# Sixteen input slabs of a hybrid decoder layer become fill work between the steps of its recurrences

## The chip, the cores and the metric

One core of a Trainium2 chip runs the whole program in one launch. The metric is device time in microseconds; three runs of the kernel before gave a median of 2457.02 us (2455.21 to 2465.17).

## The reference, cut to what matters

Two layers over 512 prompt tokens and 8 decode tokens (520 columns, always carried together). A layer first mixes tokens:

```python
h = rmsnorm(x, norm1_g)
z = h @ w_in                                   # 57 column groups of 128 here
mq, mk, mv, mi, mf, mo, gq, gk, gv, glr, go, pu, gates = split_cols(z)
hm, C1, n1, m1 = mlstm_chunked(q, k, v, i_pre, logf, C0, n0, m0)   # needs mq mk mv mi mf
y_ml  = head_rmsnorm(hm, ml_g) * sigmoid(mo)
og, S1 = gla_chunked(q2, k2, v2, log_a, S0)                        # needs gq gk gv glr
y_gla = head_rmsnorm(og, gla_g) * silu(go)
y_pool, buf1 = pool_mixer(pu, buf0, pos0, pool_w, pool_scale)      # needs pu
proj  = einsum('btnc,ncd->btnd', stack([y_ml, y_gla, y_pool]), w_branch)
x = x + sum(sigmoid(gates) * proj) @ w_out
```

and then channels: a dense SwiGLU in layer 0, a top-2-of-8 mixture of experts in layer 1. All is float32.

## The kernel before, in words

Activations lie with the feature on the partition and the 520 tokens along the free axis. A weight is streamed from HBM in slabs of 1024 by 128 (512 KB). ScalarE copies a slab to a rounded part `w_hi` (`split_hi`), VectorE subtracts to get the remainder `w_lo` (`split_lo`), and TensorE forms hi*hi + hi*lo + lo*hi, that is 48 matmuls of 260 columns per slab, into one of two PSUM places (`out_ps`). There are four places for raw slabs and three for split ones, and a slab is split two slabs ahead of its use. SyncE loads the slabs, in order, and stores the gates (below) in between.

The 57 slabs of `w_in` come in this order: 1 with the small gates and the low-rank part, 2 gk, 2 gq, 4 gv, then 4 q, 4 k, 4 v, 4 pooling inputs, then 32 gates (mo, go, 24 branch gates). Before, the first 25 run back to back (`inputs`): VectorE reads each result from PSUM, multiplies it by the row norm `rs` and writes its buffer. The remaining 32 are *fill slabs*: in the program of every engine a call `fill(k)` stands between the steps of the recurrences and does k half slabs of its share of the work. On TensorE that is 24 matmuls; on ScalarE, at every second half, the split of the slab two ahead and the copy of the slab before it out of PSUM into `sq`; on VectorE the subtraction. SyncE stores `sq` to DRAM (`gates_kept`); later GpSimd reloads the gates six at a time and VectorE scales them (`gate_scale`).

The order of a layer is written out by hand, the same on each engine: `inputs`, the GLA chunks, GLA decode, the mLSTM row scalars and its four heads, between them the pooling on GpSimd (a head's pooled product closes each mLSTM head on TensorE), four heads of mLSTM decode, `head_norm` (sums of squares of 8 tiles by a product with ones), `gates` (norm, gate and split of the branches), `merge` (12 branch slabs, then 8 of `w_out`), the channel mix. TensorE calls fill for 26 halves in GLA and its decode, 4 before the mLSTM heads, 7 in each head, so 58 by the start of mLSTM decode; there 4 a head stand, of which the first 6 use up the 64 halves that there are.

Of the kernel before, what the change touches and what calls it, by code (L numbers as in the profile page):

```python
# [17 lines left out]
ALU = mybir.AluOpType  # L18
# [32 lines left out]

N_GATES = 2 * H + 3 * KT
S_BRANCH = Z_MO + N_GATES
S_OUT = S_BRANCH + KT // 2 * 3
# [105 lines left out]
def decoder(nc, slabs, x_in, vectors, if_bias, gate_w, pool_w, consts, ml_m0, ml_n0, ml_C0,  # L160
# [194 lines left out]
    gain_diag_ready, gain_row_ps, gain_row_ready = sem("gain_diag"), sem("gain_row_ps"), sem("gain_row")  # L355
    act_scaled, gate_done = sem("act_scaled"), sem("gate_done")
    h_hi_ready, h_lo_ready = sem("h_hi_ready"), sem("h_lo_ready")

# [75 lines left out]
    def gate_slab(f):  # L434

        return 3 * f - 1 if f else 0

    def gate_back(l, k):
# [96 lines left out]
    def _(pool):  # L535
# [33 lines left out]
        for l in range(DEPTH):  # L569
# [19 lines left out]
            pool.dma_start(ext[:, :, :, 0:POOL_BUF], pool_in[l]).then_inc(pool_loaded, 16)  # L589
            pool.wait_ge(*evac(l * O_LAYER1 + Z_MO - 1))  # L590
            pool.wait_ge(*evac(l * O_LAYER1 + Z_MO - 2))
            pool.dma_start(pool_u[l], br[:, 8:12, NP_TOK - POOL_BUF:T]).then_inc(st_pu, 16)
# [101 lines left out]
    def _(act):  # L694
# [31 lines left out]
        def inputs(l, nb, ob):  # L726

            for i in range(Z_MO):
                n, o = nb + i, ob + i
                split_hi(n + 2)  # L730
                if i == 0:
                    norm(2 * l)
                    act.wait_ge(loaded, 32)
                    act.wait_ge(small_scaled, 2 * (l + 1))
                    nc.scalar.activation(row_i[:], row_i[:], ACT.Identity,
                                         bias=ifb[:, l, 0:1]).then_inc(rows.sem, 1)
                    nc.scalar.activation(row_f[:], row_f[:], ACT.Identity,
                                         bias=ifb[:, l, 1:2]).then_inc(rows.sem, 1)
# [46 lines left out]
        def mlstm(l):  # L785
# [38 lines left out]
            for h in range(H):  # L824
                fill(4)

# [7 lines left out]
        def head_norm(l):  # L834

            act.wait_ge(ds.sem, ds.after("h", H * l + H - 1))
            for t in range(9):
                if t < 8:
                    i = 8 * l + t
                    if t >= 2:  # L840
                        act.wait_ge(hn_ssq, i - 1)
                    nc.scalar.activation(sq[:, t % 2], br[:, t], ACT.Square).then_inc(hn_sq, 1)
                if t == 1:
                    for s, n in mixers_done(l):
                        act.wait_ge(s, n)
                if t > 0:
                    b, i = (t - 1) % 2, 8 * l + t - 1
                    act.wait_ge(hn_ssq, i + 1)
                    nc.scalar.activation(halves(mixed[:, t - 1]), ps[:, 4 + 2 * b:6 + 2 * b, 0:HALF],
                                         ACT.Ln, bias=eps, scale=1.0 / P).then_inc(hn_ln, 1)  # L850
            act.wait_ge(hn_ln, 8 * (l + 1))
            for t in range(0, 8, 2):
                nc.scalar.activation(mixed[:, t:t + 2], mixed[:, t:t + 2], ACT.Exp,  # L853
                                     scale=-0.5).then_inc(hn_rs, 1)

        def fill(k):

            for _ in range(k):
                i, half = divmod(fills[0], 2)
                fills[0] += 1  # L860
                if half or i >= N_GATES:
                    continue
                split_hi(fills[1] * LAYER1 + Z_MO + i + 2)
                if i > 0:
                    gate_out(fills[1], i - 1)

        def gate_out(l, i):

            n, o = l * LAYER1 + Z_MO + i, l * O_LAYER1 + Z_MO + i
            out_done(n)  # L870
            if i >= 2:
                act.wait_ge(*gate_kept(l, i - 2))
            nc.scalar.activation(halves(sq[:, i % 2]), out_ps(o), ACT.Copy).then_inc(emptied[o % 2], 1)

        def filled(l):

            fill(2 * N_GATES - fills[0])
            gate_out(l, N_GATES - 1)
            for i in range(2):
                act.wait_ge(*gate_kept(l, N_GATES - 2 + i))  # L880

        def gate_sigmoid(l, k):

            act.wait_ge(gate_scaled, N_GATES * l + k + 1)
            at = gate_back(l, k)[0]
            if H <= k < 2 * H:
                if k >= H + 2:
                    act.wait_ge(gated, 2 * H * l + k - 1)
                to = sq[:, k % 2]
            else:  # L890
                to = gs[:, at]
            nc.scalar.activation(to, gs[:, at], ACT.Sigmoid).then_inc(gate_sig, 1)

        def gates(l):
            for k in range(AHEAD):
                gate_sigmoid(l, k)
            for j in (8, 9, 10, 11, 0, 1, 2, 3, 4, 5, 6, 7):
# [3 lines left out]
                if j < 8:  # L901
                    gate_sigmoid(l, j + AHEAD)

        def merge(l, nb, ob):
# [15 lines left out]
            for m in range(KT):  # L920
                split_hi(nb + S_OUT + m + 2)
                gained_hi(2 * l + 1, m, evac(ob + O_OUT + m))
                square(2 * l + 1, m)
# [117 lines left out]
        for l in range(DEPTH):  # L1041
# [4 lines left out]
            mlstm(l)  # L1046
            filled(l)
            head_norm(l)
            gates(l)
            merge(l, nb, ob)  # L1050
            if l == 0:
# [14 lines left out]
    def _(dve):  # L1066
# [31 lines left out]
        def inputs(l, nb, ob):  # L1098
            for i in range(Z_MO):
                n, o = nb + i, ob + i  # L1100
# [10 lines left out]
                for first, last, buf, at, scale in ((Z_GK, Z_GQ, gk, 0, None), (Z_GQ, Z_GV, gq, 0, DK ** -0.5),  # L1111
                                                    (Z_GV, Z_Q, gv, 0, None), (Z_Q, Z_K, q, 0, None),
                                                    (Z_K, Z_V, k, 0, P ** -0.5), (Z_V, Z_PU, v, 0, None),
                                                    (Z_PU, Z_MO, br, 8, None)):
                    if first <= i < last:
# [171 lines left out]
        def mlstm_decode(l):  # L1287
            dve.wait_ge(st_C, 16 * H * (l + 1))
            dve.wait_ge(st_nm, 48 * (l + 1))
            for h in range(H):  # L1290
                rep, C_h = H * l + h, Cs[:, h % 2]
# [41 lines left out]
                dve.wait_ge(reciprocals_spread, rep + 1)  # L1333
                inc(tt_op(br[:, h, NP_TOK:T], num8[:], ps[:, 4, 0:NS_TOK], ALU.mult))

        def fill(k):

            for _ in range(k):
                i, half = divmod(fills[0], 2)
                fills[0] += 1  # L1340
                if half or i >= N_GATES:
                    continue
                split_lo(fills[1] * LAYER1 + Z_MO + i + 2)

# [8 lines left out]
        def gates(l):  # L1353
# [5 lines left out]
            for k in range(2 * H):  # L1359
# [8 lines left out]
                dve.wait_ge(gate_sig, N_GATES * l + k + 1)  # L1368
                tt_op(br[:, k], br[:, k], sq[:, k % 2] if k >= H else gs[:, at], ALU.mult).then_inc(gated, 1)
                gate_scale(l, k + AHEAD)  # L1370
                if 0 < k <= H:
                    dve.wait_ge(br_hi_ready, 12 * l + 4 + k)
                    tt_op(br_lo[:, k - 1], br[:, k - 1], br_hi[:, k - 1].bitcast(F32),
                          ALU.subtract).then_inc(br_lo_ready, 1)

        def merge(l, nb, ob):
# [277 lines left out]
        for l in range(DEPTH):  # L1654
# [7 lines left out]
            mlstm_decode(l)  # L1662
            fill(2 * N_GATES - fills[0])
            gates(l)
# [15 lines left out]
    def _(pe):  # L1680
# [47 lines left out]
        def gla(l, ob):  # L1728
            pe.wait_ge(ggw_in, 16 * (l + 1))
            pe.wait_ge(*evac(ob + Z_SMALL))  # L1730
            pe.wait_ge(*evac(ob + Z_MO - 1))
            pe.wait_ge(*evac(ob + Z_MO - 2))
            for j in range(2):
# [67 lines left out]
        def mlstm(l):  # L1801
# [12 lines left out]
            pe.wait_ge(rows.sem, rows.after("turned", l))  # L1814
            pe.wait_ge(st_Ss, 32 * (l + 1))
            for h in range(H):
                rep = H * l + h
# [41 lines left out]
        def mlstm_decode(l):  # L1859
            pe.wait_ge(po.sem, po.after("y3", l))  # L1860
            for h in range(H):
# [15 lines left out]
                at("add")  # L1877
                exact(ps[:, 4, 0:NS_TOK], ones[0:NS_TOK], rdiag[:]).then_inc(reciprocals_spread, 1)

        def head_norm(l):  # L1880
            pe.wait_ge(po.sem, po.after("y3", l))
            for t in range(8):
# [4 lines left out]
                for hf in range(2):  # L1887
                    ins = exact(ps[:, 4 + 2 * (t % 2) + hf, 0:HALF], ones,
                                sq[:, t % 2, HALF * hf:HALF * (hf + 1)])
                ins.then_inc(hn_ssq, 1)  # L1890

        def fill(k):

            for _ in range(k):
                i, half = divmod(fills[0], 2)
                fills[0] += 1
                if i >= N_GATES:
                    continue
                n, o = fills[1] * LAYER1 + Z_MO + i, fills[1] * O_LAYER1 + Z_MO + i
                if not half:  # L1900
# [154 lines left out]
        for l in range(DEPTH):  # L2055
            nb, ob = l * LAYER1, l * O_LAYER1
            for i in range(Z_MO):
                slab_to_out(nb + i, ob + i, h_hi, h_lo, None if i else (h_lo_ready, 2 * l))
# [7 lines left out]
            mlstm_decode(l)  # L2066
            fill(2 * N_GATES - fills[0])
            head_norm(l)
            merge(l, nb, ob)
            if l == 0:  # L2070
# [155 lines left out]
```

## Time and profile before

| | us |
|---|---|
| median of the runs | 2457.02 |
| the profiled execution, its own time | 2456.44 |
| its span, first to last instruction | 2454.6 |
| TensorE busy | 2195.4 (89%) |
| VectorE, ScalarE, GpSimd busy | 1325.5, 921.2, 443.0 |
| mean granted TensorE clock | 0.936 |

The page cuts the span in 40 slices of some 61 us. Layer 0 mixes tokens up to about 690 us, layer 1 from 1066 to about 1720 us; the experts fill the rest.

### The profile page before, as it was taken

What the parts mean: (1) busy time and instruction counts of PE and PEld (TensorE: products, weight loads), DVE (VectorE), ACT (ScalarE), POOL (GpSimd) and SP (SyncE); (2) the same over time, 40 slices, a digit from 0 to 9 for tenths busy, and PEclk for the clock granted to TensorE, in tenths of its full rate; (3) what the DMA queues carried; (4) which work ended last, traced back from release to release, by engine and by line L of the source; (5) the groups of instructions that cost most, each with busy time, mean ns of one, the idle gap of its engine ahead of it and who ended that gap; (6) DMA issues with size and microseconds to landing.
All of it is one profiled execution on the core that took longest, in us unless ns stands there. A gap on an engine that the chain in (4) does not pass through costs nothing.

```text
span 2454.6 us, 38904 instructions
## 1 busy us (share of the span) xinstructions
PE 2195.4 (89%) x15621; PEld 2014.7 (82%) x15621; DVE 1325.5 (54%) x1872; ACT 921.2 (38%) x1262; POOL 443.0 (18%) x387
## 2 busy tenths in 40 slices
PE   6999999739999999999999997389599999999993
PEld 6999887428999999999998874289588888887883
DVE  4344433656645543343443446575476777777775
ACT  4123232053333322221322320533355555555556
POOL 0000122031000000000001220310334433444343
PEclk9999999669999999999999996699699999999996
DMA  4223422225622232322234222242377767776775
GB/s 158 95 84 104 143 81 85 99 73 153 255 87 92 89 95 87 95 89 93 95 106 122 90 93 82 83 145 86 137 228 236 235 226 228 229 233 227 232 232 169
DMA packets 102639, 341.76 MB, mean 139 GB/s; under 512 B 13129, under 2 KB 17257, under 8 KB 102249
## 3 DMA queue, kind: packets, MB, share of 16 engines
q1 hardware_dynamic: 85416, 278.46, 35.3%
q0 software_dynamic: 15568, 56.34, 6.8%
q10 hardware_dynamic: 1536, 5.24, 0.6%
q8 instruction: 92, 1.51, 0.2%
q14 instruction: 27, 0.21, 0.0%
HBM read 294.28 MB, written 46.17 MB: 139 GB/s over the span
## 4 chain that ended last, share of the span: by engine, by line
PE 58%; issue 20%; POOL 11%; DVE 5%; ACT 4%; DMA 2%; POOLq 0%; ACTq 0%; DVEq 0%; SPq 0%
PE ps L1691 47%; POOL w_lo L658 9%; PE ps L1685 9%; ACT w_hi L700 1%; POOL br_lo L627 1%; DVE gt L1397 1%; DVE mixed L1402 1%; DVE gs L1351 0%; POOL token_slots L673 0%; ACT mixed L853 0%; DVE Cq L1328 0%; DVE Cs L1326 0%; DVE num L1331 0%; DMA raw<-slabs 0%; DVE mixed L1397 0%
## 5 line engine op out<-in xcount | busy, mean ns | idle before, releaser
L700 ACT ACTIVATE w_hi<-raw 128x1024 fp32r<-128x1024 f32 x488 | 513.3, 1054 | 498.3 <-PE ps L1691 426.0
L1076 DVE TENSOR_TENSOR w_lo<-raw,w_hi 128x1024 fp32r<-128x1024 f32 x383 | 473.6, 1237 | 235.2 <-ACT w_hi L700 232.0
L1691 PE MATMUL ps<-h_hi,w_hi 128*128 128x260 f32 x2544 | 530.9, 290 | 20.8 <-DVE h_lo L1085 13.6
L1691 PE MATMUL ps<-h_hi,w_lo 128*128 128x260 f32 x2544 | 518.1, 286 | 0.0
L1691 PE MATMUL ps<-h_lo,w_hi 128*128 128x260 f32 x2544 | 517.9, 286 | 0.0
L1691 PEld LDWEIGHTS ps<-h_hi,w_hi 128*128 128x128 f32 x2544 | 400.8, 192 | 40.3 <-issue 23.4
L2013 PE MATMUL ps<-hg,w_hi 128*128 128x320 f32 x1408 | 378.7, 351 | 27.7 <-POOL w_lo L658 25.3
L1691 PEld LDWEIGHTS ps<-h_lo,w_hi 128*128 128x128 f32 x2544 | 398.3, 192 | 0.0
L1691 PEld LDWEIGHTS ps<-h_hi,w_lo 128*128 128x128 f32 x2544 | 398.1, 191 | 0.0
L2015 PE MATMUL ps<-hg,w_lo 128*128 128x160 f32 x1408 | 337.6, 240 | 0.0
L658 POOL TENSOR_TENSOR w_lo<-raw,w_hi 128x1024 fp32r<-128x1024 f32 x105 | 250.1, 2385 | 396.1 <-ACT w_hi L700 395.8
L2013 PEld LDWEIGHTS ps<-hg,w_hi 128*128 128x128 f32 x1408 | 269.6, 191 | 39.1 <-POOL w_lo L658 28.0
L2015 PEld LDWEIGHTS ps<-hg,w_lo 128*128 128x128 f32 x1408 | 274.5, 195 | 3.2
L1691 PE MATMUL ps<-br_hi,w_hi 128*128 128x260 f32 x384 | 83.0, 299 | 86.6 <-issue 56.3
L1691 PEld LDWEIGHTS ps<-br_hi,w_hi 128*128 128x128 f32 x384 | 63.3, 202 | 90.8 <-issue 68.5
L2027 PE MATMUL ps<-w_hi,ma_parts 128*128 128x512 f32 x352 | 116.3, 412 | 6.1 <-POOL w_lo L658 5.5
L1598 DVE TENSOR_TENSOR ma<-gsum,msig 128x160 f32<-128x160 f32 x88 | 80.0, 909 | 52.4 <-ACT msig L994 52.4
L1596 DVE TENSOR_REDUCE gsum<-ps 128x160 f32<-128x320 f32 x88 | 43.1, 490 | 85.4 <-PE ps L2015 85.2
L578 POOL DMA_DIRECT2D S_p<-S x2 | 1.2, 598 | 455.8 <-DVE S L1180 455.8
L1691 PE MATMUL ps<-br_lo,w_hi 128*128 128x260 f32 x384 | 81.5, 295 | 0.0
L1691 PE MATMUL ps<-br_hi,w_lo 128*128 128x260 f32 x384 | 81.2, 295 | 0.0
L575 POOL DMA_DIRECT2D m_s<-ml_m x2 | 1.1, 546 | 430.0 <-DVE x L1463 430.0
(357 smaller groups left out, 3042.4 us busy)
## 6 DMA issues: line engine op xcount, KB each, us to landing
raw<-slabs SPq DMA_DIRECT2D x489, 512.0 KB, 3.6
gates_kept<-sq SPq DMA_DIRECT2D x64, 260.0 KB, 2.1
gs<-gates_kept POOLq DMA_DIRECT2D x64, 260.0 KB, 3.2
token_slots<-zeros POOLq DMA_DIRECT2D x1, 9600.0 KB, 34.8
rows_in<-token_slots POOLq DMA_DIRECT2D x9, 512.0 KB, 5.4
Cs<-ml_C POOLq DMA_DIRECT2D x8, 512.0 KB, 3.9
C_s<-Cs POOLq DMA_DIRECT2D x8, 512.0 KB, 2.9
token_slots<-yt ACTq DMA_DIRECT2D x8, 512.0 KB, 2.7
```

What stands on the lines that cost most here:

```text
L627: nc.gpsimd.tensor_tensor(br_lo[:, t], br[:, t], br_hi[:, t].bitcast(F32), ALU.subtract).then_inc(br_lo_gpsimd, 1)
L658: nc.gpsimd.tensor_tensor(w_lo[:, n % SPL], raw[:, place(n)], w_hi[:, n % SPL].bitcast(F32), ALU.subtract).then_inc(lo_ready_gpsimd, 1)
L700: nc.scalar.activation(w_hi[:, n % SPL], raw[:, place(n)], ACT.Copy).then_inc(hi_ready, 1)
L1076: tt_op(w_lo[:, n % SPL], raw[:, place(n)], w_hi[:, n % SPL].bitcast(F32), ALU.subtract).then_inc(lo_ready, 1)
L1397: tt_op(halves(to), out_ps(o), halves(gs[:, at]), ALU.mult).then_inc(emptied[o % 2], 1)
L1596: nc.vector.tensor_reduce(gsum[:], addends(b), AX.X, ALU.add).then_inc(m_sum, 1)
L1598: tt_op(ma[:, f % 2], gsum[:], msig[:], ALU.mult).then_inc(m_gate, 1)
L1685: return mm(out, a, b, start=start, stop=stop, skip_group_check=True)
L1691: ins = mm(out[:, hf], wgt_part[:, slot, tile], in_part[:, kk, HALF * hf:HALF * (hf + 1)], start=first and not ends and in_part is in_hi, ...
L2013: mm(out[:, 0:2 * CAP], w_hi[:, (s0 + s) % SPL, kk], hg[:, kk], start=kk == 0, stop=False, skip_group_check=True)
L2015: ins = mm(out[:, 0:CAP], w_lo[:, (s0 + s) % SPL, kk], hg[:, kk, 0:CAP], start=False, stop=kk == KT - 1, skip_group_check=True)
L2027: mm(ps[:, 4 + hf_], parts[:, at:at + P], w[:, slot_n, 4 * hf_:4 * hf_ + 4], start=f == 0 and a == 0, stop=f == FE_TILES - 1 and a == 2)
```

## The change

The first 9 slabs stay in `inputs`; q, k, v and the pooling inputs (16 slabs) become fill slabs ahead of the 32 gates, so 48 fill slabs, 96 halves. ScalarE copies these 16 from PSUM unscaled straight into `q`, `k`, `v` and `br`; VectorE multiplies each in place by `rs` (k by its factor too) two fill slabs later and counts them in `qkvu_scaled`. TensorE waits for 12 of them before the mLSTM heads, VectorE before mLSTM decode, GpSimd for all 16 before it stores and pools the pooling inputs. The calls of fill before mLSTM decode stay as they are; then there are 5 halves per decode head (4 before), 4 in `head_norm`, and the remaining 14 stand on TensorE behind `head_norm` and on ScalarE and VectorE as `fill(2)` in each step of `gates`. `head_norm` uses `q` for its squares and the silu gates use `mixed`, since `sq` still carries gates; the wait for the last two gate stores moves into `merge`.

```diff
+N_QKVU = Z_MO - Z_Q
+N_FILL = N_QKVU + N_GATES
@@ gpsimd
-            pool.wait_ge(*evac(l * O_LAYER1 + Z_MO - 1))
-            pool.wait_ge(*evac(l * O_LAYER1 + Z_MO - 2))
+            pool.wait_ge(qkvu_scaled, N_QKVU * (l + 1))
             pool.dma_start(pool_u[l], br[:, 8:12, NP_TOK - POOL_BUF:T])
@@ scalar
-            for i in range(Z_MO):
+            for i in range(Z_Q):
@@ mlstm, for the decode heads
-                fill(4)
+                fill(5)
@@ head_norm
-                    nc.scalar.activation(sq[:, t % 2], br[:, t], ACT.Square).then_inc(hn_sq, 1)
+                    nc.scalar.activation(q[:, t % 2], br[:, t], ACT.Square).then_inc(hn_sq, 1)
+                    if t % 2:
+                        fill(1)
@@ fill
-                if half or i >= N_GATES:
+                if half or i >= N_FILL:
                     continue
-                split_hi(fills[1] * LAYER1 + Z_MO + i + 2)
+                split_hi(fills[1] * LAYER1 + Z_Q + i + 2)
                 if i > 0:
-                    gate_out(fills[1], i - 1)
+                    fill_out(fills[1], i - 1)
+        def fill_out(l, i):
+            n, o = l * LAYER1 + Z_Q + i, l * O_LAYER1 + Z_Q + i
             out_done(n)
+            gate = i - N_QKVU
+            if gate >= 2:
+                act.wait_ge(*gate_kept(l, gate - 2))
+            to = qkvu(i) if gate < 0 else sq[:, gate % 2]
+            nc.scalar.activation(halves(to), out_ps(o), ACT.Copy).then_inc(emptied[o % 2], 1)
@@ gates
                 if j < 8:
                     gate_sigmoid(l, j + AHEAD)
+                    fill(2)
@@ vector, fill
+                if 2 <= i < 2 + N_QKVU:
+                    qkvu_scale(fills[1], i - 2)
+        def qkvu_scale(l, i):
+            dve.wait_ge(*evac(l * O_LAYER1 + Z_Q + i))
+            if H <= i < 2 * H:
+                ins = stt_op(qkvu(i), qkvu(i), P ** -0.5, rs[:, 0], ALU.mult, ALU.mult)
+            else:
+                ins = tt_op(qkvu(i), qkvu(i), rs[:, 0], ALU.mult)
+            ins.then_inc(qkvu_scaled, 1)
@@ vector, after mlstm_decode
-            fill(2 * N_GATES - fills[0])
+            fill(4)
@@ vector, gates, at the end of a step
+                fill(2)
@@ tensor, mlstm
             pe.wait_ge(st_Ss, 32 * (l + 1))
+            pe.wait_ge(qkvu_scaled, N_QKVU * l + 3 * H)
@@ tensor, mlstm_decode, at the end of a head
+                fill(1)
@@ tensor, head_norm
+                if t % 2:
+                    fill(1)
@@ tensor
-            fill(2 * N_GATES - fills[0])
             head_norm(l)
+            fill(2 * N_FILL - fills[0])
             merge(l, nb, ob)
```

## Rows read from the trace of the kernel before

**Rows 1.** The page: clock in slices, and the chain by engine.

```profile
PEclk9999999669999999999999996699699999999996
...
PE 58%; issue 20%; POOL 11%; DVE 5%; ACT 4%; DMA 2%; POOLq 0%; ACTq 0%; DVEq 0%; SPq 0%
```

**Rows 2.** Busy time by stretch: length, each engine with instructions, granted clock, DMA.

```profile
33.00:168.00 135.00, 134.82 (x1104) 134.61 (x1104) 45.55 (x48) 25.65 (x25) 0.00 (x0) 0.98 0.30 94
...
428.00:448.00 20.00, 19.42 (x111) 16.04 (x112) 12.01 (x19) 2.50 (x3) 1.77 (x4) 0.83 0.40 133
465.00:495.00 30.00, 18.20 (x27) 7.71 (x28) 17.43 (x31) 1.16 (x2) 2.12 (x4) 0.50 0.13 49
...
507.00:549.00 42.00, 5.20 (x26) 4.92 (x25) 27.01 (x32) 21.64 (x32) 16.41 (x16) 0.60 0.15 45
1549.00:1590.00 41.00, 4.93 (x25) 4.75 (x25) 27.09 (x32) 20.73 (x31) 16.27 (x16) 0.59 0.16 46
549.00:621.00 72.00, 65.63 (x504) 64.20 (x504) 50.16 (x69) 25.44 (x37) 10.16 (x19) 0.95 0.47 144
```

**Rows 3.** Timeline of ScalarE in the inputs: start, duration, work, idle before.

```profile
156.38 1.06 ACT L700 ACTIVATE w_hi<-raw 128x1024 fp32r<-128x1024 f32 x1 [4.70 <-PE ps L1691]
162.15 1.06 ACT L700 ACTIVATE w_hi<-raw 128x1024 fp32r<-128x1024 f32 x1 [4.71 <-PE ps L1691]
```

**Rows 4.** Lines: count, busy us, mean ns, idle before them.

```profile
L700 ACT ACTIVATE w_hi<-raw 128x1024 fp32r<-128x1024 f32 x488 | 513.3, 1054 | 498.3 <-PE ps L1691 426.0 <-DMA raw<-slabs 45.5 <-PE ps L2031 14.8
L1076 DVE TENSOR_TENSOR w_lo<-raw,w_hi 128x1024 fp32r<-128x1024 f32 x383 | 473.6, 1237 | 235.2 <-ACT w_hi L700 232.0
...
L1351 DVE TENSOR_TENSOR gs<-gs,rs 128x520 f32<-128x520 f32 x64 | 47.2, 741 | 26.2 <-DMA gs<-gates_kept 26.2
L873 ACT ACTIVATE sq<-ps 128x520 f32<-128x520 f32 x64 | 37.7, 589 | 11.0 <-PE ps L1691 11.0
...
L900 ACT ACTIVATE br_hi<-br 128x520 fp32r<-128x520 f32 x24 | 14.2, 624 | 12.6 <-DVE br L1369 12.6
```

**Rows 5.** Timeline of VectorE at the end of layer 0's first mLSTM head.

```profile
318.47 0.69 DVE L1283 TENSOR_TENSOR br<-ps,den 128x512 f32<-128x512 f32 x1
319.08 1.22 DVE L1076 TENSOR_TENSOR w_lo<-raw,w_hi 128x1024 fp32r<-128x1024 f32 x1
```

**Rows 6.** Timeline of GpSimd: layer 0's first pooling.

```profile
276.82 0.79 POOL L592 DMA_DIRECT2D pool_u<-br  x1
282.49 0.81 POOL L595 COPY ext<-br 128x32 f32<-128x32 f32 x1 [4.88 <-DMA ext<-pool_in]
...
289.76 0.20 POOL L565 TENSOR_TENSOR pd<-pred,br 128x8 f32<-128x8 f32 x1
```

**Rows 7.** Chain of waits in order of time, layer 0: start, us, what.

```profile
319.21 1.15 PE ps L1685 x4
...
428.06 0.27 PE ps L1865
...
434.27 4.47 PE ps L1685 x8
438.74 8.21 PE ps L1691 x48
...
447.79 0.27 PE ps L1865
...
448.29 5.77 PE ps L1691 x48
...
492.11 0.17 DVE br L1334
...
505.97 1.16 PE ps L1685 x4
...
514.41 2.22 ACT gs L892 x4
...
548.86 4.99 PE ps L1691 x24
```

More of the change, by code:

```diff
@@ L356, in decoder @@
     act_scaled, gate_done = sem("act_scaled"), sem("gate_done")
+    qkvu_scaled = sem("qkvu_scaled")
     h_hi_ready, h_lo_ready = sem("h_hi_ready"), sem("h_lo_ready")
@@ L436, in gate_slab, with qkvu @@
         return 3 * f - 1 if f else 0
+    def qkvu(i):
+        return ((q, k, v)[i // H][:, i % H] if i < 3 * H else br[:, 8 + i - 3 * H])
     def gate_back(l, k):
@@ L860, in fill @@
                 fills[0] += 1
-                if half or i >= N_GATES:
+                if half or i >= N_FILL:
                     continue
-                split_hi(fills[1] * LAYER1 + Z_MO + i + 2)
+                split_hi(fills[1] * LAYER1 + Z_Q + i + 2)
                 if i > 0:
-                    gate_out(fills[1], i - 1)
-        def gate_out(l, i):
-            n, o = l * LAYER1 + Z_MO + i, l * O_LAYER1 + Z_MO + i
+                    fill_out(fills[1], i - 1)
+        def fill_out(l, i):
+            n, o = l * LAYER1 + Z_Q + i, l * O_LAYER1 + Z_Q + i
             out_done(n)
-            if i >= 2:
-                act.wait_ge(*gate_kept(l, i - 2))
-            nc.scalar.activation(halves(sq[:, i % 2]), out_ps(o), ACT.Copy).then_inc(emptied[o % 2], 1)
+            gate = i - N_QKVU
[3 more added lines that the diff above has]
+            nc.scalar.activation(halves(to), out_ps(o), ACT.Copy).then_inc(emptied[o % 2], 1)
         def filled(l):
-            fill(2 * N_GATES - fills[0])
-            gate_out(l, N_GATES - 1)
-            for i in range(2):
-                act.wait_ge(*gate_kept(l, N_GATES - 2 + i))
+            fill(2 * N_FILL - fills[0])
+            fill_out(l, N_FILL - 1)
         def gate_sigmoid(l, k):
@@ L886, in gate_sigmoid @@
             if H <= k < 2 * H:
-                if k >= H + 2:
-                    act.wait_ge(gated, 2 * H * l + k - 1)
-                to = sq[:, k % 2]
+                to = mixed[:, k - H]
             else:
@@ L921, in merge @@
                 split_hi(nb + S_OUT + m + 2)
+                if m < 2:
+                    act.wait_ge(*gate_kept(l, N_GATES - 2 + m))
                 gained_hi(2 * l + 1, m, evac(ob + O_OUT + m))
@@ L1046, in _ @@
             mlstm(l)
-            filled(l)
             head_norm(l)
             gates(l)
+            filled(l)
             merge(l, nb, ob)
@@ L1098, in inputs @@
         def inputs(l, nb, ob):
-            for i in range(Z_MO):
+            for i in range(Z_Q):
                 n, o = nb + i, ob + i
@@ L1111, in inputs @@
                 for first, last, buf, at, scale in ((Z_GK, Z_GQ, gk, 0, None), (Z_GQ, Z_GV, gq, 0, DK ** -0.5),
-                                                    (Z_GV, Z_Q, gv, 0, None), (Z_Q, Z_K, q, 0, None),
-                                                    (Z_K, Z_V, k, 0, P ** -0.5), (Z_V, Z_PU, v, 0, None),
-                                                    (Z_PU, Z_MO, br, 8, None)):
+                                                    (Z_GV, Z_Q, gv, 0, None)):
                     if first <= i < last:
@@ L1289, in mlstm_decode @@
             dve.wait_ge(st_nm, 48 * (l + 1))
+            dve.wait_ge(qkvu_scaled, N_QKVU * l + 3 * H)
             for h in range(H):
@@ L1340, in fill @@
                 fills[0] += 1
-                if half or i >= N_GATES:
+                if half or i >= N_FILL:
                     continue
-                split_lo(fills[1] * LAYER1 + Z_MO + i + 2)
+                split_lo(fills[1] * LAYER1 + Z_Q + i + 2)
+                if 2 <= i < 2 + N_QKVU:
[7 more added lines that the diff above has]
+            ins.then_inc(qkvu_scaled, 1)
         def gate_scale(l, k):
@@ L1368, in gates @@
                 dve.wait_ge(gate_sig, N_GATES * l + k + 1)
-                tt_op(br[:, k], br[:, k], sq[:, k % 2] if k >= H else gs[:, at], ALU.mult).then_inc(gated, 1)
+                tt_op(br[:, k], br[:, k], mixed[:, k - H] if k >= H else gs[:, at], ALU.mult).then_inc(gated, 1)
                 gate_scale(l, k + AHEAD)
@@ L1374, in gates @@
                           ALU.subtract).then_inc(br_lo_ready, 1)
+                fill(2)
+            fill(2 * N_FILL - fills[0])
         def merge(l, nb, ob):
@@ L1730, in gla @@
             pe.wait_ge(*evac(ob + Z_SMALL))
-            pe.wait_ge(*evac(ob + Z_MO - 1))
-            pe.wait_ge(*evac(ob + Z_MO - 2))
+            pe.wait_ge(*evac(ob + Z_Q - 1))
+            pe.wait_ge(*evac(ob + Z_Q - 2))
             for j in range(2):
@@ L1888, in head_norm @@
                     ins = exact(ps[:, 4 + 2 * (t % 2) + hf, 0:HALF], ones,
-                                sq[:, t % 2, HALF * hf:HALF * (hf + 1)])
+                                q[:, t % 2, HALF * hf:HALF * (hf + 1)])
                 ins.then_inc(hn_ssq, 1)
+                if t % 2:
+                    fill(1)
         def fill(k):
@@ L1896, in fill @@
                 fills[0] += 1
-                if i >= N_GATES:
+                if i >= N_FILL:
                     continue
-                n, o = fills[1] * LAYER1 + Z_MO + i, fills[1] * O_LAYER1 + Z_MO + i
+                n, o = fills[1] * LAYER1 + Z_Q + i, fills[1] * O_LAYER1 + Z_Q + i
                 if not half:
@@ L2056, in _ @@
             nb, ob = l * LAYER1, l * O_LAYER1
-            for i in range(Z_MO):
+            for i in range(Z_Q):
                 slab_to_out(nb + i, ob + i, h_hi, h_lo, None if i else (h_lo_ready, 2 * l))
@@ L2066, in _ @@
             mlstm_decode(l)
-            fill(2 * N_GATES - fills[0])
             head_norm(l)
+            fill(2 * N_FILL - fills[0])
             merge(l, nb, ob)
```

## The prediction

> **What bounds the kernel now.** I read the page first: TensorE is busy for most of the span and carries 58% of the chain that ended last, but the clock line has two hollows, one in each layer, where the granted clock falls to 0.6 [rows 1]. Then I cut each layer into its stages and asked for busy times [rows 2]. The inputs are TensorE alone: 134.82 us busy of 135.00, and ScalarE's split of a slab waits 4.7 us for TensorE each time, at a pace of 162.15 - 156.38 = 5.77 us a slab [rows 3]. The end of the token mix is the opposite. From 465 to 495 us (decode heads 2 and 3) TensorE shows 18.20 us of 30 with the clock at 0.50, and from 507 to 549 (norm and gates) 5.20 us of 42; the second layer repeats it, 4.93 of 41 [rows 2]. The reason stands in the program: the 64 halves of fill are used up in decode head 1, and behind it TensorE has only the short products of decode and norm. So work moved from the first stage to the last is paid in full in one and partly free in the other. I work out one layer and double it.
>
> **What is removed.** 16 slabs leave the inputs: 16 x 5.77 = **-92.3 us**. Their VectorE evacuation goes with them, beside TensorE and free. The same 32 halves reappear behind the old last fill, because the fill calls before mLSTM decode are the same in number; there the 48 matmuls of a slab are now q, k, v and so on, and the gates come 32 halves later. The first gate stores and reloads come later too, but gate 25 to 31, the last ones, are wanted only at the end of merge.
>
> **Scaling.** Each moved slab gets one extra VectorE multiply in SBUF; the same shape on the reloaded gates takes 0.741 us [rows 4]. ScalarE's copy (0.589) takes the place of a gate's copy. It never waits: VectorE's subtraction for slab i+2 already follows ScalarE's copy of slab i-2. In the GLA chunks VectorE waits longer than this for ScalarE and TensorE, so these cost nothing; without that cover the 16 would cost 16 x 0.74 = 11.9 us. Two stand in the chain of the mLSTM row scalars, for which TensorE waits: **+1.5** (bounds 0 and 1.5).
>
> **A new wait: pooling.** GpSimd pooled group 0 long before TensorE asked for it. Now it waits for 16 scalings, and the sixteenth stands in VectorE's last fill call of mLSTM head 0, behind the subtraction of 319.08 [rows 5], so ends about 319.08 + 1.22 + 0.74 = 321.0. Queued behind it on GpSimd are the store of `pool_u` (0.79 us to issue) and the whole of the first pooling, 282.49 to 289.96, 7.5 us [rows 6]. That ends at 329.3, while TensorE reaches the pooled product at 319.21 [rows 7]: 10.1 us in which TensorE, and behind it ScalarE's output of group 0 and the next head, stand still. The first slab after may run slowly, as one did after the decode product: 8.21 against 5.77 us, so 2.4 [rows 7]; I add 2. **+12** (bounds 0 and 14). The later groups have a whole head each and stay hidden.
>
> **Decode.** Head 0 of before is a head with four fill halves: 428.06 to 447.79, 19.7 us [rows 7]. It ran 4.47 us of products with 8 rows, and the next slab at 8.21 instead of 5.77. With a fifth half (2.88) a head is 22.6, VectorE's part lying under it (12.01 us busy in the 20 [rows 2]): 4 x 22.6 = 90.4 against 428.06 to 492.28, 64.2, so **+26.2**. Without the slow slab it is 4 x 20.2 (+16.4); with a second slow slab in each head 4 x 25.0 (+36). I take what head 0 shows.
>
> Here the Trainium skill differs. The row: the slab that begins at 438.74 ran slowly although TensorE was busy for 19.42 of the 20 us around it [rows 2, 7]. The skill (TensorE: Matmul & The Clock Gate, Part 1: The HAM clock gate) says that the gate gives full rate by how busy TensorE has been and halves it after idleness; by that a dense head would stay at 2.4 GHz and the sum would fall by 4 x 2.4 x 2 = 19 us, an estimate. I go by the row; the other is part of a rival.
>
> **Head norm.** A tile's sum of squares takes 1.16 us and after each second tile comes a half: 4 x (2.32 + 2.88) = 20.8, against 492.28 to 507.13 = 14.9: **+6** (bounds +1, if ScalarE's pace hides the halves, and +9, with ScalarE's two extra splits and copies, 2 x 1.64 [rows 4], on the chain).
>
> **Gates.** Let T0 be the end of `head_norm` on TensorE. Before, from there (507.13) to the second product of merge (548.86) were 41.7 us [rows 7]. Now 14 halves stand there. Slab 41 starts at once. Slab 42 needs the PSUM place of slab 40, and ScalarE copies that only in gate step 0: the four sigmoids ended 9.5 us after the sums before (516.63 - 507.13), now 6.6 after T0 since a half stands last; then five `br_hi` copies and a sigmoid at 0.62, a split at 1.05, the copy at 0.59 [rows 4]: T0 + 12.0, so a 6 us hole. Then six slabs, 34.6, the first half of merge 2.9, and 2.4 for a slow slab: T0 + 51.9, **+10.2**. For this the gate steps must keep up with 5.77 us a slab; a step has the old VectorE and ScalarE work and 2.88 us more (split 1.05, copy 0.59, subtraction 1.24). Bounds: with no hole 7 x 5.77 + 2.9 = 43.3 (+1.6); with the loop as the bound 6.6 + the old 32.2 + 7 x 2.88 = 59 (+17.3).
>
> **Merge** then starts warm: 504 matmuls took 65.63 us at a clock of 0.95 [rows 2], at 5.77 per 48 they take 60.6: **-5** (bounds -11, the whole idle time too, and 0).
>
> **Sum.** -92.3 + 1.5 + 12 + 26.2 + 6 + 10.2 - 5 = -41.4 a layer, -83 for two. Against the profiled execution's own 2456.4 us (span 2454.6; the median of the runs is 2457.0, 0.6 more): **2374 us**. All low bounds together give about -86 a layer (2284), all high ones -14 (2427).
>
> **Rivals.**
> 1. *The late stages take the slabs more easily.* No slow slab in decode (as the skill's rule has it), no hole in the gates, or pooling less late. For it: the next head's slab ran at 5.77 in 448.29 [rows 7]. Against: 438.74. With 20 to 26 us more over two layers: about 2350; with all, 2320.
> 2. *The gate loop becomes the bound*, ScalarE and VectorE handing splits and gates to each other in every step. For it: 27.01 and 21.64 us busy of 42 already, with 32 instructions each [rows 2]. At 8 us a step instead of 5.8: 7 x 2.2 = 15 a layer, 2405.
> 3. *Slower: the clock stays down.* Decode, head norm and gates mix 8-row products and holes into the fill, and all 38 halves from decode on run at 1.2 GHz, as 465 to 495 did [rows 2]. A half then costs about 2.3 us more: 38 x 2.3 - 9.6 already counted = +78 a layer, net +37, about 2530. It turns the sign from 18 such halves a layer. Against: the slab of 448.29, between two such products, at full rate, and the inputs at 0.98.
> 4. *It doesn't do what it says*: no idle time is filled, decode and gates lengthen by what is moved, and the time stays at 2450 to 2465. Against: the 18.20 of 30 and 5.20 of 42 us.
>
> **Chances.** Forecast (2355 to 2393) 0.52; rival 1 0.19; rival 2 0.18; rival 3 0.06; rival 4 0.05. The range 2335 to 2412 takes in the forecast and most of rivals 1 and 2, and leaves out about 0.2; the likeliest case's own range is 2355 to 2393. A measurement here tells about 0.5%, 12 us, from no change: faster 0.90, same 0.04, slower 0.06.
>
> **What would show it.** Right: inputs of 9 slabs at 5.77; TensorE waiting about 10 us for `pd` at the end of mLSTM head 0 in each layer and in no later head; decode heads of about 22.6 us; a hole of some 6 us on TensorE before the second gate-stage slab, ended by ScalarE's copy, and after it dense work to merge; two clock hollows gone from the page. Wrong: 1.2 GHz through decode fill, TensorE waiting for `w_lo` in every gate step, or recurrences longer by more than 15 us before decode.

## The result, and where the time went

The changed kernel takes 2358.24 us (median of 4 runs, 2355.95 to 2363.34), against 2458.99 for the kernel before in the same comparison: ratio 0.9591, interval 0.9563 to 0.9618. The forecast was 2374, range 2335 to 2412. The profiled execution took 2363.34 us, span 2361.3.

The page after, first engine line and clock in slices. The two hollows of [rows 1] are gone; six eights are left.

```profile
PE 2186.1 (93%) x15621; PEld 2020.7 (86%) x15621; DVE 1310.9 (56%) x1872; ACT 937.2 (40%) x1294; POOL 435.3 (18%) x387
...
PEclk9998998999999999999989989998899999999996
```

Busy time by stretch of layer 0 after, columns as in [rows 2]: decode, norm and gates, merge.

```profile
351.00:435.00 84.00, 83.66 (x531) 72.32 (x532) 50.65 (x78) 15.13 (x20) 5.35 (x10) 0.90 0.41 141
435.00:505.00 70.00, 64.37 (x495) 62.93 (x494) 37.05 (x47) 44.82 (x65) 19.08 (x22) 0.95 0.50 162
505.00:581.00 76.00, 69.51 (x553) 67.99 (x552) 54.05 (x75) 26.50 (x37) 9.86 (x18) 0.98 0.49 150
```

TensorE is now busy for 83.66 of 84 us in decode and 64.37 of 70 in norm and gates, where [rows 2] shows 18.20 of 30 and 5.20 of 42. Stage by stage, between the same instructions in both timelines (us):

| | layer 0 before | after | layer 1 before | after |
|---|---|---|---|---|
| to the first GLA product | 168.81 | 77.59 | 145.94 | 53.67 |
| GLA, to the row scalars on TensorE | 116.97 | 117.13 | 117.02 | 117.07 |
| to the first pooled product | 33.43 | 45.05 | 36.39 | 45.26 |
| to mLSTM decode | 108.85 | 111.57 | 108.90 | 111.04 |
| decode, to the first sum of squares | 65.10 | 83.85 | 66.64 | 83.77 |
| norm and gates, to the first read in merge | 57.02 | 69.71 | 57.09 | 70.14 |
| merge, to the first `w_out` product | 76.81 | 75.96 | 76.76 | 76.22 |
| sum | 626.99 | 580.86 | 608.74 | 557.17 |

(Layer 1 begins at VectorE's last write of `x` in layer 0's channel mix, before at 1059.3 us. From layer 0's first `w_out` product to there, most of it the dense SwiGLU and not the experts, it is 432.3 us in both kernels.) That is 46.1 and 51.6 us. From the last `x` of layer 1's mixer on, this execution is 4.4 us longer than before (743.0 against 738.6); the executions below have 737 to 745 there, with the same code, so that is no part of the change. The profiled execution of the changed kernel is the slowest of its four, 5.1 us above their median, so a gain read from the stages comes out some us larger than one read from the medians.

**The new wait.** Timelines of VectorE, GpSimd and TensorE after, at the end of layer 0's first mLSTM head (bracket: idle before, and what ended it):

```profile
230.97 1.22 DVE L1085 TENSOR_TENSOR w_lo<-raw,w_hi 128x1024 fp32r<-128x1024 f32 x1
232.10 0.69 DVE L1362 TENSOR_TENSOR br<-br,rs 128x520 f32<-128x520 f32 x1
...
233.09 0.76 POOL L598 DMA_DIRECT2D pool_u<-br  x1 [47.37 <-DVE br L1362]
...
239.41 0.21 POOL L572 TENSOR_TENSOR pd<-pred,br 128x8 f32<-128x8 f32 x1
...
239.77 2.07 PE L1707 MATMUL ps<-pd,pw 128*128 128x260 f32 x4 [8.70 <-POOL pd L572]
```

GpSimd sits for 47.37 us until the sixteenth scaling (232.10), then pools, and TensorE stands still for 8.70 us; in layer 1 for 8.68. [rows 6, 7] had the pooling finished 29 us before its use.

**Decode.** The chain of waits after, layer 1's second and third decode heads:

```profile
1361.27 5.77 PE ps L1713 x48
1367.04 3.94 PE ps L1707 x8
1370.98 8.69 PE ps L1713 x48
...
1379.98 3.07 PE ps L1713 x24
...
1383.38 5.77 PE ps L1713 x48
1389.15 3.63 PE ps L1707 x8
1392.78 7.46 PE ps L1713 x48
```

A full slab at full rate (5.77), eight matmuls of 8 rows, a slow slab (8.69, 7.46), half a slab: what [rows 7] showed for one head is now the pattern of all eight (7.20 to 8.69). The granted clock over layer 0's decode is 0.90, so part of it runs at 1.2 instead of 2.4 GHz. Heads are 22.15, 20.60, 20.56, 20.55 us in layer 0 and 20.52, 22.11, 20.57, 20.57 in layer 1.

**The hole in the gates.** Timelines after of ScalarE and TensorE behind head norm:

```profile
458.55 2.22 ACT L898 ACTIVATE gs<-gs 128x520 f32<-128x520 f32 x4
460.68 2.72 ACT L906 ACTIVATE br_hi<-br 128x520 fp32r<-128x520 f32 x5
463.31 0.62 ACT L898 ACTIVATE mixed<-gs 128x520 f32<-128x520 f32 x1
463.84 1.04 ACT L706 ACTIVATE w_hi<-raw 128x1024 fp32r<-128x1024 f32 x1
464.78 0.58 ACT L883 ACTIVATE sq<-ps 128x520 f32<-128x520 f32 x1
...
465.51 0.77 PE L1713 MATMUL ps<-h_hi,w_hi 128*128 128x260 f32 x2 [5.63 <-ACT sq L883]
```

ScalarE copies slab 40 out of PSUM only behind four sigmoids, five `br_hi`, one more sigmoid and a split; TensorE waits 5.63 us for that copy, in both layers. After it TensorE runs dense into merge:

```profile
465.00:505.00 40.00, 39.49 (x315) 39.52 (x316) 29.99 (x38) 19.19 (x29) 12.18 (x14) 0.95 0.62 195
```

### The profile page after: what moved, and what is told of

Same layout as the page of the kernel before. It is cut to its first block and busy times, and to the rows that moved or that the text cites. A ratio compares the mean times of both kernels' runs of the same rounds, so it can differ in the third digit from the quotient of the medians.

```text
span 2361.3 us, 38934 instructions
## 1 busy us (share of the span) xinstructions
PE 2186.1 (93%) x15621; PEld 2020.7 (86%) x15621; DVE 1310.9 (56%) x1872; ACT 937.2 (40%) x1294; POOL 435.3 (18%) x387
## 5 line engine op out<-in xcount | busy, mean ns | idle before, releaser
L1713 PE MATMUL ps<-h_hi,w_hi 128*128 128x260 f32 x2544 | 540.5, 294 | 32.0 <-DVE h_lo L1094 13.6
L1713 PE MATMUL ps<-h_hi,w_lo 128*128 128x260 f32 x2544 | 523.7, 288 | 0.0
L1713 PE MATMUL ps<-h_lo,w_hi 128*128 128x260 f32 x2544 | 523.5, 288 | 0.0
L1713 PEld LDWEIGHTS ps<-h_hi,w_hi 128*128 128x128 f32 x2544 | 407.4, 195 | 57.9 <-issue 40.0
L1713 PEld LDWEIGHTS ps<-h_lo,w_hi 128*128 128x128 f32 x2544 | 404.3, 194 | 0.0
L1713 PEld LDWEIGHTS ps<-h_hi,w_lo 128*128 128x128 f32 x2544 | 404.2, 194 | 0.0
L1003 ACT ACTIVATE msig<-gsum 128x160 f32<-128x160 f32 x88 | 29.7, 338 | 122.5 <-DVE gsum L1618 122.3
L2053 PEld LDWEIGHTS ps<-w_hi,ma_parts 128*128 128x128 f32 x352 | 61.7, 195 | 17.6 <-issue 7.4
```

Source lines behind the costliest of these rows:

```text
L1003: nc.scalar.activation(msig[:], gsum[:], ACT.Sigmoid).then_inc(m_sig, 1)
L1713: ins = mm(out[:, hf], wgt_part[:, slot, tile], in_part[:, kk, HALF * hf:HALF * (hf + 1)], start=first and not ends and in_part is in_hi, ...
L2053: mm(ps[:, 4 + hf_], parts[:, at:at + P], w[:, slot_n, 4 * hf_:4 * hf_ + 4], start=f == 0 and a == 0, stop=f == FE_TILES - 1 and a == 2)
```

## The experiments

Ratios are against the kernel before, run beside each experiment (medians 2461.45 us for the first four, 2463.18 for the other four). Stages are measured as in the table above and compared with the changed kernel there.

**Late fill undone.** The 18 halves from head norm on stand ahead of it.

```diff
 # scalar, and likewise on the tensor and vector engines
+            filled(l)
             head_norm(l)
             gates(l)
-            filled(l)
 # head_norm and gates: the calls fill(1) and fill(2) are out
```

> The 18 halves of fill that stand in head norm and behind it run back to back between decode and head norm instead; all else as in the changed kernel. Theory (the moved slabs gain because they fill TensorE time that was idle in norm and gates): these stages go back to 14.9 + 41.7 us and 9 x 5.77 = 52 us of dense slabs stand ahead of them, 108.6 against 67.9 us in the changed kernel: +41 us a layer, 2440 us, ratio 0.992. Rival (the gain lies in the fill work inside the recurrences and decode, where the late part stands makes no difference): 2355 to 2375, ratio 0.96.

2434.38 us, ratio 0.9882 (0.9858 to 0.9906). Of the change's 4.1% only 1.2% is left; the forecast of 2440 holds within 6 us and the rival falls. Busy time by stretch in layer 0: the 18 halves, then norm, then gates.

```profile
435.00:490.00 55.00, 52.79 (x431) 52.03 (x430) 13.47 (x13) 16.26 (x23) 3.27 (x6) 1.00 0.48 164
489.00:505.00 16.00, 6.87 (x25) 4.06 (x24) 0.76 (x1) 15.15 (x21) 0.00 (x0) 0.90 0.00 1
505.00:542.00 37.00, 8.81 (x42) 8.63 (x43) 30.09 (x34) 15.87 (x27) 17.86 (x17) 0.55 0.24 68
```

In the last stretch TensorE has 8.81 us of 37 at 0.55: the hollow is back as soon as the fill doesn't reach into the gates. Decode and gates together are 83.85 + 69.71 = 153.56 us after and 137.35 + 52.16 = 189.51 here: 36 us a layer, 41 expected.

**Pooling inputs ahead of the values.**

```diff
-        return ((q, k, v)[i // H][:, i % H] if i < 3 * H else br[:, 8 + i - 3 * H])
+        return (q[:, i % H], k[:, i % H], br[:, 8 + i % H], v[:, i % H])[i // H]
-            pool.wait_ge(qkvu_scaled, N_QKVU * (l + 1))
+            pool.wait_ge(qkvu_scaled, N_QKVU * l + 3 * H)
             for h in range(H):
+                pe.wait_ge(qkvu_scaled, N_QKVU * l + 3 * H + h + 1)
-        ... (mq, 4), (mk, 4), (mv, 4), (pu, 4), ...
+        ... (mq, 4), (mk, 4), (pu, 4), (mv, 4), ...
```

Two more edits belong to it: TensorE's wait for 12 scalings ahead of the heads is out, and VectorE waits for all 16 before mLSTM decode.

> The pooling inputs come ahead of the values in the fill slabs, GpSimd waits for 12 scalings instead of 16, and TensorE waits for a head's own values at the head. Theory (TensorE's 8.7 us wait for pd at the end of mLSTM head 0 comes only from the sixteenth scaling): that wait is gone in both layers, and the slow slab behind it, 9 to 11 us a layer, 2338 us, ratio 0.951. Rival (GpSimd's pooling then runs beside VectorE's row scalars and split, both slow each other on SBUF, and the time comes back there): pd wait gone but the rows and head 0 longer by 5 us or more, 2350 us or above.

2344.29 us, ratio 0.9524 (0.9500 to 0.9548), 6 us above what was expected. TensorE and GpSimd in layer 0:

```profile
191.93 0.76 POOL L598 DMA_DIRECT2D pool_u<-br  x1 [7.27 <-DVE br L1362]
...
199.15 0.21 POOL L572 TENSOR_TENSOR pd<-pred,br 128x8 f32<-128x8 f32 x1
...
230.23 1.14 PE L1707 MATMUL ps<-pd,pw 128*128 128x260 f32 x4
```

The pooling starts 41 us earlier and no idle time stands ahead of the pooled product. From the row scalars to decode the layer falls from 156.62 to 144.63 us (layer 1: 156.30 to 144.63), 12 us; GLA grows by 0.8. So the wait and the slow slabs behind it were nearly the whole of that term; the rival's 5 us don't appear. The medians show 14 us of the 23 of both layers: 5 is the profiled execution of the changed kernel, and 3.6 were lost outside the mixers, where the code is the same.

**One fill step ahead of the gate sigmoids.**

```diff
         def gates(l):
+            fill(2)
             for k in range(AHEAD):
                 gate_sigmoid(l, k)
```

> ScalarE does one of its fill steps (a split and the copy of slab 40 out of PSUM) ahead of the gate sigmoids instead of in gate step 0. Theory (the 5.6 us hole of TensorE behind the first slab after head norm comes from that copy standing behind five splits and five sigmoids): the hole is gone, the gate phase 4 to 5.6 us shorter a layer, 2347 to 2350 us, ratio 0.956. Rival (the hand-over between ScalarE and VectorE bounds the gate steps, the sigmoids 1.6 us later push the first gate and all behind it): the hole moves to a later slab or to the start of merge, no change, 2356 to 2362.

2349.79 us, ratio 0.9536 (0.9510 to 0.9563). The same place in TensorE's timeline:

```profile
468.48 0.48 PE L1714 MATMUL ps<-h_hi,w_hi 128*128 128x260 f32 x2 [1.31 <-ACT sq L883]
```

The hole is 1.31 us, one slab later, behind the next copy. Norm and gates go from 69.71 to 65.10 (70.14 to 65.48 in layer 1), merge gains 1.7. The theory holds, but for these 1.31 us: the hole moved one slab on, as the rival said, at a quarter of its size. Its cause is not the rival's hand-over: on ScalarE four sigmoids, five `br_hi`, a sigmoid, a split and this copy stand back to back from 461.51 us on, with no wait for VectorE among them.

```profile
467.75 0.59 ACT L883 ACTIVATE sq<-ps 128x520 f32<-128x520 f32 x1
```

**Decode products split by half a slab.**

```diff
                 for c in range(2):
                     exact(ps[:, 4 + c], tok8[:, 0], diag[:, 0, 4 * c:4 * c + 4])
+                fill(1)
                 for c in range(2):
                     ins = exact(ps[:, 6 + c], ones[0:NS_TOK], diag[:, 1, 4 * c:4 * c + 4])
                 ins.then_inc(outer_done, 1)
-                fill(2)
+                fill(1)
```

> In each mLSTM decode head half a slab of fill stands between the two pairs of 8-row products instead of behind both. Theory (the slab behind these products runs at 7.5 to 8.7 instead of 5.77 us because products of 8 rows, back to back, let the granted clock fall): the slow slab goes or is half as slow, 1 to 2 us a head, 8 to 16 us in all, 2342 to 2350, ratio 0.954. Rival (any mixture with these products lowers the clock by the same amount): heads of 20.6 to 22 us as in the changed kernel, 2356 to 2362.

2353.01 us, ratio 0.9557 (0.9533 to 0.9580), which overlaps the changed kernel's interval and lies between the theory's 2350 and the rival's 2356; the stage shows more than the total. Chain of waits, a head of layer 1:

```profile
1356.98 5.77 PE ps L1713 x48
1362.75 1.91 PE ps L1707 x4
1364.66 3.07 PE ps L1713 x24
1367.73 1.91 PE ps L1707 x4
1369.64 3.06 PE ps L1713 x24
```

The same 48 matmuls take 3.07 + 3.06 = 6.13 us instead of 7.46 or 8.69. Heads are 19.4 us, below the rival's 20.6 to 22, but the last one of each layer still had slow halves (22.50 in layer 0, 20.93 in layer 1); why only that one stays open. Decode is 3.1 and 4.5 us shorter, just under the 8 us in all that the theory asked for.

**VectorE evacuates the 16 slabs itself.** ScalarE's copy and the second pass are gone.

```diff
-                if 2 <= i < 2 + N_QKVU:
-                    qkvu_scale(fills[1], i - 2)
+                if 1 <= i < 1 + N_QKVU:
+                    qkvu_scale(fills[1], i - 1)
-                ins = tt_op(qkvu(i), qkvu(i), rs[:, 0], ALU.mult)
+                ins = tt_op(halves(qkvu(i)), out_ps(o), halves(rs[:, 0]), ALU.mult)
-            ins.then_inc(qkvu_scaled, 1)
+            ins.then_inc(emptied[o % 2], 1)
```

> The 16 moved slabs are read from PSUM and scaled by VectorE in one step, one fill slab after their product, as in the inputs before; ScalarE's copy and VectorE's second pass are gone, all fill calls stay. Theory (copying by ScalarE and scaling later gains nothing by itself and costs the pooling wait, since the sixteenth scaling comes a fill slab later than a direct evacuation): no wait for pd, GLA and rows as in the changed kernel, 9 to 11 us a layer less, 2338 to 2342, ratio 0.952. Rival (with one engine to empty PSUM the recurrences' own VectorE steps stand behind TensorE's slabs): GLA to rows longer than 117.1 by 5 us or more a layer, 2350 or above.

2344.50 us, ratio 0.9511 (0.9483 to 0.9539). Waits of TensorE from GLA to the rows of layer 0 (us in total, times, longest):

```profile
PE ps L1717 <- DVE br L1366: 4.6, 1, 4.6
```

The time lies between the two forecasts, and both theories are half right. No wait for the pooling is left, and one new wait of 4.6 us stands between the two slabs ahead of the row scalars, since VectorE empties PSUM only behind their chain. GLA to rows grows to 122.74 and 124.03, past the rival's 5 us, but the next stage falls from 45.05 to 31.31 us (45.26 to 32.88 in layer 1), since the pooling wait is gone and the row scalars are further on when TensorE gets there. So the ScalarE copy does have a use: with it TensorE waits for no evacuation of a fill slab in this region.

**Scaling on 8 columns.** `qkvu_scale` with `[:, 0:8]` on its operands.

> The 16 scalings work on 8 of the 520 columns, so q, k, v and the pooling inputs stay unscaled in the rest; all waits and counts stay. Theory (the scalings are hidden but for the sixteenth ahead of the pooling and one or two in the row scalars): from the row scalars to the first pooled product 1 to 1.5 us less than the 45.05 and 45.26 us of the changed kernel, GLA as before, 2 to 4 us in all. Rival (VectorE is short of time in the recurrences, so 16 scalings cost most of their 11 us): 8 us or more a layer less, spread over GLA, rows and heads.

2348.91 us in a single run. Row scalars to the pooled product fall by 3.4 and 3.6 us, GLA by 0.6 and 0.4: 8 us in all, twice the theory's upper end and half of what the rival asked for. TensorE's waits in the changed kernel, then in this one:

```profile
PE ps L1707 <- POOL pd L572: 8.7, 1, 8.7
PE ps L1845 <- DVE w3b L1256: 1.7, 1, 1.7
PE ps L1828 <- ACT w L802: 0.7, 1, 0.7
```

```profile
PE ps L1707 <- POOL pd L572: 8.2, 1, 8.2
PE ps L1845 <- DVE w3b L1256: 1.2, 1, 1.2
```

The waits shrink by 1.7 us. The rest shows in the products behind them: from its start to the next product the slab after the row scalars took 7.87 and 8.15 us (layers 0 and 1) in the changed kernel and 7.36 and 7.38 here, and the short products ahead of it ran faster too. But the length of the wait alone doesn't settle this: in the kernel before that slab took 7.17 and 8.49 us, behind the same wait of 1.1 us in both layers.

**All three repairs in one.** Pooling inputs first, one early fill step, split decode products.

> Pooling inputs ahead of the values, one fill step ahead of the gate sigmoids and the decode products split by half a slab, all in one. Theory (three separate waits, each in its own place): the gains add up, by stage 11.5 + 5.5 + 4 = 21 us a layer under the changed kernel, 2312 to 2325 us, ratio 0.943. Rival (behind the removed waits the ScalarE to VectorE hand-over or the split bounds instead): 2330 or above.

2322.62 us, ratio 0.9428 (0.9405 to 0.9450): faster than both kernels, 5.7% under before and 1.7% under the change (0.9428 / 0.9591 = 0.983, from two comparisons). Layer 0 is 580.86 - 559.13 = 21.7 us shorter, layer 1 20.4, where the three alone give 19.9 and 21.0: they add up, and the rival's 2330 is not reached. Decode, then norm and gates, of layer 0:

```profile
342.00:422.00 80.00, 80.00 (x534) 67.87 (x533) 49.21 (x76) 17.25 (x23) 3.81 (x8) 0.98 0.43 151
422.00:485.00 63.00, 61.04 (x485) 59.63 (x484) 41.95 (x46) 42.74 (x63) 21.02 (x22) 1.00 0.53 172
```

**The same with VectorE's evacuation** in place of the pooling inputs ahead of the values:

> As three_together, but in place of the pooling inputs ahead of the values VectorE evacuates the 16 slabs directly. Theory: within 4 us of three_together, 2312 to 2325, ratio 0.943, since both end the wait for the pooling and nothing else differs. Rival (VectorE waiting for TensorE in the recurrences): slower than three_together by 8 us or more.

2329.08 us, ratio 0.9455 (0.9430 to 0.9480). The medians differ by 6.5 us, more than the theory's 4, but the intervals overlap, so these runs don't order the two, and a gap of 8 us is not shown. The stages put it behind by 3.9 and 2.0 us, as the 4.6 us wait would have it.

## Why the prediction was right

- *Inputs, -92.3 a layer*: -91.2 and -92.3.
- *Scaling, +1.5*: right in place (the row scalars), but by the run with 8 columns it is nearer to 4 us a layer, 0.5 of them in the wait for the pooling: more of the short products and of the slab behind the row scalars run slowly. Against the kernel before, the stages up to the pooled product grew, without the 8.7 us of waiting, by 3.1 us in layer 0 and 0.2 in layer 1, where that slab had been slow already; what starts the slow stretch there stays open.
- *Pooling, +12*: the mechanism, its place and its end were right; 8.70 us of waiting for 10.1, because GpSimd's copy and subtraction ran at 0.36 and 1.26 us with VectorE idle, against 0.81 and 2.33 before, beside VectorE's subtractions. The stage grew by 11.6 and 8.9, scaling included, and the next one by 2.7 and 2.1, for which 2 had been added.
- *Decode, +26.2*: the term that was mis-sized. It is +18.8 and +17.1. The mechanism, a slow slab behind the 8-row products, holds in all eight heads. But I took head 0 of before, with 4.47 us for these products and 8.21 for the slab, for all; one head in each layer is like it (22.15 and 22.11 us, where the forecast said 22.6), and the other six take 20.5 to 20.6, their products mostly 3.63 and their slab 7.20 to 7.48. Over both layers that is 16.5 us, as much as the whole forecast was high. That the other misses nearly cancel is luck: norm and gates were 6.7 us too high over both layers, merge 8.6 too low.
- *Norm and gates, +6 and +10.2*: +12.7 and +13.1 together, 3 us a layer under the forecast, with the hole at the predicted slab and for the predicted reason (5.63 us, forecast 6). The gate steps kept up.
- *Merge, -5*: -0.9 and -0.5. I read busy time as if it were the pace. TensorE waits for VectorE's reads of its branch products in both kernels, the same 4.7 + 1.6 us (before, then after):

```profile
PE ps L1691 <- DVE gt L1397: 4.7, 2, 2.3
PE ps L1691 <- DVE mixed L1397: 1.6, 2, 0.8
...
PE ps L1713 <- DVE gt L1419: 4.7, 2, 2.4
PE ps L1713 <- DVE mixed L1419: 1.6, 2, 0.8
```

  The kernel before ran two stretches of its merge at half rate in layer 0: from 548.86 to 552.93 us, which ends 2.8 us behind the first read, and from 586.77 to 590.53, behind a wait of 2.34 us for such a read. Only the first is gone. Behind the same wait the changed kernel has one again (540.64 to 544.10), so a warm start doesn't bring all 504 matmuls to 5.77 us per 48. Behind that wait the granted clock, third from the end, is 0.52 before and 0.50 after:

```profile
587.00:590.00 3.00, 3.00 (x16) 3.00 (x16) 2.89 (x5) 0.68 (x2) 1.02 (x2) 0.52 0.51 169
...
541.00:544.00 3.00, 3.00 (x16) 3.00 (x15) 2.75 (x5) 0.82 (x2) 0.88 (x2) 0.50 0.49 152
```

  What would shorten merge was not tried.
- *Rivals*: the time lies inside the forecast's own range, near its lower end and nearer to rival 1's 2350 than to 2374. But of rival 1's conditions only an earlier end of the pooling came true, by 1.4 us; the slow slabs and the hole are there. Rival 2 (gate loop as the bound) is not seen, with TensorE busy for 39.49 of the 40 us behind the hole, nor rival 3 (half rate throughout), with clocks of 0.90 and 0.95; rival 4 is refuted by the late fill undone.
- *A slip*: the low bounds add up to -84.3 us a layer (2288 us), not -86.

## What to carry to other kernels

Work that can run at any time belongs where the engine that bounds the kernel stands idle, and the program has to carry it to the very end of that idle stretch: here some 70% of the gain (1.2% left of 4.1%) hung on the last 18 halves of each layer. Where such work also makes an input, follow each consumer on every engine: one count of 16 for all put a pooling that nobody had been waiting for on the path, and a reorder of four slabs took it off again. When a stage's cost is taken from one sample, look whether the sample is like the others: the decode head used here was like the slowest of four.

## What the runs showed of the hardware that was not expected

A slab behind eight 8-row matmuls in a row is slow, 7.20 to 8.69 against 5.77 us in all eight heads, although TensorE was busy for 83.66 of 84 us. In layer 0's second decode head these products run from 379.68 to 383.3 us:

```profile
380.00:384.00 4.00, 4.00 (x13) 1.81 (x12) 2.78 (x10) 0.00 (x0) 0.00 (x0) 0.97 0.47 136
384.00:387.00 3.00, 3.00 (x16) 3.00 (x15) 1.85 (x2) 0.00 (x0) 0.00 (x0) 0.50 0.00 0
```

TensorE is busy without a gap, and behind the 8-row products it runs at 1.2 GHz. Plain fp32 products as such don't do this: in the mLSTM heads 7.5 us of them (217.55 to 225.06), most with 128 rows, stand ahead of a slab, and all of it runs at 2.4 GHz:

```profile
217.50:231.00 13.50, 13.50 (x84) 10.39 (x83) 4.68 (x4) 2.46 (x5) 0.00 (x0) 1.00 0.05 20
```

With half a slab between two groups of four, six of eight heads have no half slab at the lower rate. So here the 8-row products, not idleness, took the clock down; whether by their few rows or by the zeros of their diagonal operand, no run separates. The Trainium skill (TensorE: Matmul & The Clock Gate, Part 1: The HAM clock gate) describes half rate as the state after idleness; with idleness as the profile shows it, these rows don't agree with that for products of 8 rows.
